# Second block's attention interleaved with its query and output projections

## The chip, the cores and the metric

One core of a Trainium2 chip runs the kernel in one launch. The metric is the device time of the whole program in microseconds (us). TensorE (PE) does the matrix products, VectorE (DVE) and ScalarE (ACT) the elementwise work, GpSimd (POOL) small set-up work, and SyncE (SP) issues the weight transfers.

## The reference, cut to what matters

The program computes two model blocks on 256 tokens of width 1024, in float32. The change lies in the second layer of the first block, a chunked band attention whose keys and values were computed from the residual stream:

```python
def chunk_band_attention(u, k_pad, v_pad, w_q, w_o, rel_bias):
    q = (u @ w_q).reshape(...)               # 16 heads of 64
    s = einsum('bqhd,bkhd->bhqk', qc, kb) * scale + bias
    p = softmax(where(valid, s, -1e30), axis=-1)
    o = einsum('bhqk,bkhd->bqhd', p, vb)
    return o.reshape(bsz, seq, B_DIM) @ w_o
# around it:
h = h + g1[:, None, :] * chunk_band_attention(...)
u = modulate(rms_norm(h, norm_ffn[layer]), sh2, sc2)
h = h + g2[:, None, :] * swiglu(u, ffn_w_in[layer], ffn_w_out[layer])
```

`g1`, `sh2`, `sc2` and `g2` come from one long row of sums, `silu(c) @ mod_w`, whose last parts are finished only just before they are used.

## The kernel before, in words

Activations are kept transposed, as 8 chunks of 128 features by 256 tokens. Every linear layer reads its weight in slots of 1 MB (1024 by 256) from a ring of six; SP issues slot n once slot n-6 is free. A slot is two pieces of 128 output features. To keep float32 accuracy a piece is split: ACT writes the high part (`hi_upto`, L739), DVE the low part as the difference (`lo_upto`, L1119), into one of four buffers; a buffer is free once the piece that held it is done on PE. A piece is then 24 matmuls on PE: for each of 8 chunks, high by high, high by low and low by high of the activations `u` (`linear`, L1750). `linear_pair` (L1763) does two pieces chunk by chunk, as `u` arrives. Two pieces share one of two PSUM banks (`lin`), which ACT or DVE drains before the next but one pair may start.

All engines run instructions in the order written; that order is set by hand. In the stretch of the change, PE does the 8 query pieces `b_q`, two row sums (L1814), then the heads, then the 8 output pieces `b_o`. DVE reads "row" slots in between (`weighted_rows`, L1180), which share the ring with the weights; the table `ROWS_AT` says behind which of the twelve slots of `kv_k`, `kv_v`, `b_q` a row slot stands.

One head is, on PE, the bias product and two score products (L2009, L2013) into bank 2 or 3; DVE takes the two maxima (L1424); ACT does the exponentials (L899); DVE takes the reciprocal and scales (L1433, L1436); PE transposes (L2024); ACT copies (L910); PE multiplies by the values (L2044, L2045) into bank 6 or 7, two heads to a chunk. `attention_pe` issues for step i: transposes of head i, scores of head i+2, values of head i-1, and what `between(i)` holds. `attention_dve` issues for step i: maxima of head i+1, scaling of head i, the drain of head i-3, `between(i)`. `attention_act`: exponentials of i, copy of i-1, drain of i-2, `between(i)`.

The eight result chunks are copied from PSUM to `qB` (ACT, L965), and once all are there, copied to the high half of `u` (ACT, L968), and subtracted for the low half (DVE, L1482). PE then starts `b_o` by `project`. At head 2 PE also turns the late row sums into columns (L1822).

Of the kernel before, what the change touches and what calls it, by code (L numbers as in the profile page):

```python
# [29 lines left out]
DC = D // P  # L30
T = 256
# [26 lines left out]
ROWS_AT = (2, 3, 4, 5, 6, 7, 8, 9)  # L58
# [123 lines left out]
def two_blocks(nc, x, c, mod_w, mod_b, norm_mix, norm_ffn, ffn_w_in, ffn_w_out, a_w_in, a_w_out, a_lb,  # L182
# [15 lines left out]
    with ExitStack() as ctx:  # L198
# [3 lines left out]
        def sem(name):  # L202
            return ctx.enter_context(nc.semaphore(name))
# [270 lines left out]
        def lo_before(k):  # L474

            return k - 12
# [30 lines left out]
        bo_hi, bo_lo = sem("bo_hi"), sem("bo_lo")  # L507
# [143 lines left out]
        def _(pool):  # L651
# [37 lines left out]
            pool.wait_ge(bo_lo, 8)  # L689
# [21 lines left out]
            pool.wait_ge(at_lo, 4)  # L711
# [17 lines left out]
        def _(act):  # L729
# [211 lines left out]
            for n, pair in enumerate(pairs("b_q")):  # L941
                result(pair)
                act.activation(qB[:, 2 * n:2 * n + 2, :], bank(pair), ACT.Copy, scale=0.125).then_inc(lin_out["act"], 1)
            drained = [0]
# [16 lines left out]
            act.wait_ge(rows_mm, 3)  # L961
            act.activation(late_rows, ps[:, 4:6, :], ACT.Copy).then_inc(rows_sb, 1)
            act.wait_ge(piece_done, LAST["b_q"] + 1)

            attention_act("B", lambda i, o: act.activation(qB[:, i // 2, :], o[:, 0:T], ACT.Copy))  # L965
            act.wait_ge(at_hi, HB // 2)
            for c_ in range(DC):
                act.activation(u[:, 0, c_, :], qB[:, c_, :], ACT.Copy).then_inc(bo_hi, 1)  # L968
# [142 lines left out]
        def _(dve):  # L1111
# [278 lines left out]
            def last_gains():  # L1390

                dve.wait_ge(gemv_col, 5)
                dve.tensor_tensor(mod[:, 80:112], ps[:, 0, 0:32], vec1[:, 80:112], ALU.add).then_inc(mod_done, 1)
# [82 lines left out]
            splits("b_q")  # L1476
            lo_upto(LAST["b_q"] + LOOKAHEAD)
            attention_dve("B", None)
            last_gains()
            for c_ in range(DC):  # L1480
                dve.wait_ge(bo_hi, c_ + 1)
                dve.tensor_tensor(u[:, 1, c_, :], qB[:, c_, :], u[:, 0, c_, :].bitcast(F32), ALU.subtract)\  # L1482
                    .then_inc(bo_lo, 1)
# [245 lines left out]
        def _(pe):  # L1729
# [267 lines left out]
            def attention_pe(kind, keys, queries, values, chunks, bias=None, between=lambda i: None):  # L1997
# [3 lines left out]
                def scores(i):  # L2001
# [3 lines left out]
                    elif i >= 2:  # L2005
                        pe.wait_ge(at_e, 2 * (a - 1))
                    o = ps[:, 2 + i % 2, :]
# [20 lines left out]
                def outputs(i):  # L2028
# [3 lines left out]
                    if k - {"B": 0, "W": 8, "X": 12}[kind] >= 2:  # L2032
                        pe.wait_ge(at_hi, k - 1)
                        if kind == "X":
                            pe.wait_ge(at_lo, lo_before(k - 1))
# [45 lines left out]
            linears(jobs["b_q"], (u_lo, 24))  # L2081
# [293 lines left out]
```

## Time and profile before

| | us |
|---|---|
| median of 3 runs | 1603.47 |
| lowest, highest | 1602.63, 1615.23 |
| the profiled execution | 1611.56 |
| its span, first to last instruction | 1609.6 |
| mean granted PE clock | 0.959 |

The profile is of one execution, which took 1611.56 us, 8.1 us more than the median. The rows from its trace give times from the start of the span. A clock of 1.00 is 2.4 GHz and 0.50 is 1.2 GHz; numbers between are means over a window that holds both.

### The profile page before, as it was taken

Reading aid. Unit: us, or ns where it says so; the run is one execution under the profiler, and the core shown is the slowest. Engines: PE = TensorE matmul, PEld = TensorE weight load, DVE = VectorE, ACT = ScalarE, POOL = GpSimd, SP = SyncE. Lnnn points to the kernel's source line nnn. Section 1 sums busy time; section 2 is a strip of 40 time slices with the busy share of each in tenths; the row PEclk is TensorE's granted clock in tenths of the full one; section 3 lists DMA queues with packets and bytes.
Section 4 is the critical chain, followed back from the end, with each engine's and each line's share of the span. In section 5 each row is a group of like instructions: output and inputs, shape, how many; then the busy total and the mean of one; then the engine's idle time right before and its main releaser. Section 6 shows DMA issues by size and latency. Waiting matters only on the chain.

```text
span 1609.6 us, 26565 instructions
## 1 busy us (share of the span) xinstructions
PE 1525.9 (95%) x11398; PEld 1250.1 (78%) x11398; DVE 712.9 (44%) x1137; ACT 566.0 (35%) x883; POOL 28.0 (2%) x47
## 2 busy tenths in 40 slices
PE   5899999899998989999999899989899999999997
PEld 3898899899998658999999778979656556556563
DVE  3657757766777425554446535644211111111110
ACT  1531244344444434544445735543111111212111
POOL 1000000000001001000000000001000000000000
PEclk8899999999989889999999879999999999999999
DMA  9668635989769403455554223716699999999992
GB/s 330 196 214 288 232 132 186 327 285 321 269 213 336 157 0 125 162 187 183 178 155 132 84 76 103 288 53 252 271 416 419 423 422 421 422 424 421 420 424 96
DMA packets 175635, 404.15 MB, mean 251 GB/s; under 512 B 5013, under 2 KB 139442, under 8 KB 163250
## 3 DMA queue, kind: packets, MB, share of 16 engines
q1 hardware_dynamic: 173504, 397.43, 66.6%
q0 software_dynamic: 1648, 5.18, 1.1%
q8 instruction: 77, 1.26, 0.3%
q10 hardware_dynamic: 386, 0.11, 0.0%
q14 instruction: 20, 0.16, 0.0%
HBM read 401.63 MB, written 1.07 MB: 250 GB/s over the span
## 4 chain that ended last, share of the span: by engine, by line
PE 87%; DVE 6%; DMA 3%; ACT 3%; issue 1%; SPq 0%; ACTq 0%; DVEq 0%
PE ps L1750 28%; PE ps L2268 14%; PE ps L2290 7%; PE ps L1981 7%; PE ps L1763 4%; PE ps L1785 4%; PE ps L2255 4%; PE ps L2300 4%; PE ps L2013 2%; PE ps L1914 2%; PE ps L1838 2%; DMA arena<-in_mod_w 2%; PE ps L1848 1%; DVE wsplit L1119 1%; PE ps L1805 1%; DMA arena<-in_b_w_q 1%
## 5 line engine op out<-in xcount | busy, mean ns | idle before, releaser
L1750 PE MATMUL ps<-u,wsplit 128*128 128x256 f32 x3912 | 485.3, 285 | 8.6 <-DVE wsplit L1119 7.1
L1750 PEld LDWEIGHTS ps<-u,wsplit 128*128 128x128 f32 x3912 | 477.0, 193 | 15.9 <-DVE wsplit L1119 8.1
L1119 DVE TENSOR_TENSOR wsplit<-arena,wsplit 128x1024 fp32r<-128x1024 f32 x258 | 312.6, 1224 | 250.4 <-ACT wsplit L739 247.4
L739 ACT ACTIVATE wsplit<-arena 128x1024 fp32r<-128x1024 f32 x258 | 270.6, 1056 | 332.2 <-PE ps L1750 161.4
L1676 DVE TENSOR_TENSOR arena<-arena,ps 128x256 f32<-128x256 f32 x32 | 13.5, 421 | 358.6 <-ACT arena L1085 358.6
L2268 PE MATMUL ps<-arena 128*64 128x256 f32 x1408 | 155.7, 379 | 0.8 <-DVE arena L1671 0.8
L2268 PEld LDWEIGHTS ps<-arena 128*64 128x64 f32 x1408 | 101.0, 137 | 60.6 <-issue 12.0
L1981 PE MATMUL ps<-hid,wsplit 128*128 128x256 f32 x1056 | 130.2, 283 | 0.3 <-DVE hid L1360 0.3
L1981 PEld LDWEIGHTS ps<-hid,wsplit 128*128 128x128 f32 x1056 | 128.2, 192 | 0.5 <-DVE hid L1360 0.5
L1091 ACT ACTIVATE arena<-ps 64x512 f32<-64x512 f32 x64 | 37.8, 591 | 154.0 <-PE ps L2290 153.2
L1763 PE MATMUL ps<-u,wsplit 128*128 128x256 f32 x528 | 73.6, 304 | 14.6 <-DVE u L1168 12.8
L1763 PEld LDWEIGHTS ps<-u,wsplit 128*128 128x128 f32 x528 | 71.3, 209 | 17.8 <-issue 17.0
L1785 PE MATMUL ps<-wsplit,u 128*128 128x256 f32 x672 | 85.0, 288 | 0.0
L1785 PEld LDWEIGHTS ps<-wsplit,u 128*128 128x128 f32 x672 | 83.0, 195 | 2.3 <-issue 2.3
L2290 PE MATMUL ps<-arena 128*64 128x512 f32 x352 | 80.4, 598 | 1.2 <-ACT arena L1088 1.2
L1085 ACT ACTIVATE arena<-ps 128x256 f32<-128x256 f32 x32 | 12.3, 383 | 174.5 <-PE ps L2268 174.5
L2268 PE MATMUL ps<-late,arena 128*64 128x256 f32 x640 | 70.8, 379 | 0.0
L2268 PEld LDWEIGHTS ps<-late,arena 128*64 128x64 f32 x640 | 45.9, 137 | 27.4 <-issue 5.7
L2255 PE MATMUL ps<-arena 128*128 128x128 f32 x512 | 63.8, 278 | 2.0 <-DVE arena L1659 2.0
L2255 PEld LDWEIGHTS ps<-arena 128*128 128x128 f32 x512 | 59.5, 192 | 7.8 <-issue 5.8
L2300 PE MATMUL ps<-arena 128*128 128x512 f32 x128 | 61.7, 605 | 1.3 <-ACT arena L1091 1.3
L2290 PEld LDWEIGHTS ps<-arena 128*64 128x64 f32 x352 | 23.3, 136 | 48.1 <-issue 45.3
(345 smaller groups left out, 1375.8 us busy)
## 6 DMA issues: line engine op xcount, KB each, us to landing
arena<-in_w SPq DMA_DIRECT2D x66, 2048.0 KB, 17.0
late<-in_w SPq DMA_DIRECT2D x30, 2048.0 KB, 17.2
arena<-in_mod_w SPq DMA_DIRECT2D x48, 1024.0 KB, 6.9
arena<-in_ffn_w_in SPq DMA_DIRECT2D x44, 1024.0 KB, 5.5
arena<-in_ffn_w_out SPq DMA_DIRECT2D x22, 1024.0 KB, 4.9
arena<-in_a_w_in SPq DMA_DIRECT2D x16, 1024.0 KB, 7.9
arena<-in_kv_mod_w SPq DMA_DIRECT2D x8, 1024.0 KB, 5.3
arena<-in_kv_w SPq DMA_DIRECT2D x8, 1024.0 KB, 7.2
```

What stands on the lines that cost most here:

```text
L739: act.activation(piece_buf(p, 0), piece_src(p), ACT.Copy).then_inc(hi_done, 1)
L1091: act.activation(y_sb[64 * k:64 * k + 64, 512 * j:512 * (j + 1)], ps[64 * j:64 * j + 64, 6, :], ACT.Copy).then_inc(m_yc, 1)
L1119: dve.tensor_tensor(piece_buf(p, 1), piece_src(p), piece_buf(p, 0).bitcast(F32), ALU.subtract).then_inc(lo_done, 1)
L1750: mm = pe.matmul(o, w_[:, k, :], u[:, x_, k, :], start=first, stop=last)
L1763: mm = pe.matmul(lin[p["out"] % 2][:, p["half"], :], piece_buf(p, lo)[:, k, :], u[:, x_, k, :], start=(at == 0 and n == 0 and p["half"] == 0),
L1785: mm = pe.matmul(lin[p["out"] % 2][:, b, :].rearrange("p (c n) -> p c n", c=2), u[:, x_, k, P * b:P * (b + 1)], wsplit[:, first_buf:first_ ...
L1838: mm = pe.matmul(o, sq[:, k, P * b:P * (b + 1)], of, start=(k == 0 and b == 0), stop=(k == DC - 1), skip_group_check=True)
L1981: mm = pe.matmul(acc[:, c_, :], piece_buf(p, lo)[:, k, P * jj:P * (jj + 1)], hid[:, fi % 2, x_, k, :], start=(i == 1 and c_ % 2 == 0 and k ...
L2255: mm = pe.matmul(ps[:, 6 + half, P * c_:P * (c_ + 1)], hn_tok[:, b, P * (4 * half + c_):P * (4 * half + c_ + 1)], sel[:, b, :], start=(b = ...
L2268: mm = pe.matmul(ps[64 * j:64 * j + 64, 0, 256 * m:256 * (m + 1)], xe[:, c_, own], w13[w_][:, m, c_, 256 * j:256 * (j + 1)], start=(c_ == ...
L2290: mm = pe.matmul(ps[64 * j:64 * j + 64, 6, :], tt[:, P * m + 64 * jk:P * m + 64 * jk + 64], w2b[w_][:, 2 * jk + m, 512 * j:512 * (j + 1)], ...
L2300: mm = pe.matmul(ps[:, 2 + 2 * b + j, :], tt[0:rows, 256 + P * b:256 + P * (b + 1)], y_sb[0:rows, 512 * j:512 * (j + 1)], start=False, sto ...
```

## The change

It has six parts.

1. `ROWS_AT` moves from slots 2 to 9 to slots 1 to 8.
2. PE does `b_q` pieces 0 and 1, the row sums, piece 2, the columns (now into the PSUM bank of `modps`), piece 3, the first two heads' scores, piece 4, and then pieces 5, 6 and 7 at steps 0, 1 and 2 of the heads. ACT drains the later query pairs inside the steps (1 and 3), and both split the weights inside them.
3. ACT writes a head pair's high part straight from PSUM to `u`, and DVE subtracts it from the same PSUM bank.
4. PE accumulates the first four `b_o` pieces by chunks: from step 5 on, each step holds the 6 matmuls of two pieces of one bank for one chunk (`out_chunk`).
5. Pieces 4 to 7 of `b_o` follow as whole pieces, with the sums of squares behind them.
6. The waits of PE and POOL on the results' semaphores are renumbered, since the heads now raise `at_lo`.

```diff
@@ -55,7 +55,7 @@
 VEC = {}
-ROWS_AT = (2, 3, 4, 5, 6, 7, 8, 9)
+ROWS_AT = (1, 2, 3, 4, 5, 6, 7, 8)
@@ -473,7 +473,7 @@
-            return k - 12
+            return k - 4
@@ -686,7 +685,7 @@
-            pool.wait_ge(bo_lo, 8)
+            pool.wait_ge(at_lo, 8)
             pool.memset(pair_ones, 0.0).then_inc(w_ms, 1)
@@ -708,7 +707,7 @@
-            pool.wait_ge(at_lo, 4)
+            pool.wait_ge(at_lo, 12)
             pool.memset(turned, 0.0).then_inc(m_const, 1)
@@ -938,9 +937,30 @@
             operand_hi("mix1", lambda c_: mod[:, 64 + c_:65 + c_], LAST["kv_v"])
-            for n, pair in enumerate(pairs("b_q")):
+            def queries(pair):
+                n = pairs("b_q").index(pair)
                 result(pair)
                 act.activation(qB[:, 2 * n:2 * n + 2, :], bank(pair), ACT.Copy, scale=0.125).then_inc(lin_out["act"], 1)
+            queries(pairs("b_q")[0])
+            act.wait_ge(rows_mm, 3)
+            act.activation(late_rows, ps[:, 4:6, :], ACT.Copy).then_inc(rows_sb, 1)
+            queries(pairs("b_q")[1])
+            def amid_b(i):
+                if i == 0:
+                    hi_upto(jobs["b_q"][7]["w"])
+                elif i in (1, 3):
+                    queries(pairs("b_q")[(i + 3) // 2])
+                elif i == 4:
+                    hi_upto(jobs["b_o"][3]["w"])
+            def out_hi(i, o):
+                if i == 1:
+                    act.wait_ge(piece_done, LAST["b_q"] + 1)
+                return act.activation(u[:, 0, i // 2, :], o[:, 0:T], ACT.Copy)
             drained = [0]
@@ -958,14 +978,7 @@
-            act.wait_ge(rows_mm, 3)
-            act.activation(late_rows, ps[:, 4:6, :], ACT.Copy).then_inc(rows_sb, 1)
-            act.wait_ge(piece_done, LAST["b_q"] + 1)
-            attention_act("B", lambda i, o: act.activation(qB[:, i // 2, :], o[:, 0:T], ACT.Copy))
-            act.wait_ge(at_hi, HB // 2)
-            for c_ in range(DC):
-                act.activation(u[:, 0, c_, :], qB[:, c_, :], ACT.Copy).then_inc(bo_hi, 1)
+            attention_act("B", out_hi, amid_b)
             hi_upto(jobs["b_o"][0]["w"] + LOOKAHEAD)
@@ -1390,7 +1403,7 @@
                 dve.wait_ge(gemv_col, 5)
-                dve.tensor_tensor(mod[:, 80:112], ps[:, 0, 0:32], vec1[:, 80:112], ALU.add).then_inc(mod_done, 1)
+                dve.tensor_tensor(mod[:, 80:112], modps[:, 80:112], vec1[:, 80:112], ALU.add).then_inc(mod_done, 1)
                 dve.wait_ge(mod_done, 11)
@@ -1473,14 +1486,20 @@
                 dve.tensor_copy(memT[:, 4 * b:4 * b + 4, :], acc[:, 4 * b:4 * b + 4, :]).then_inc(x_tc, 1)
-            splits("b_q")
-            lo_upto(LAST["b_q"] + LOOKAHEAD)
-            attention_dve("B", None)
+            lo_upto(jobs["b_q"][1]["w"])
+            weighted_rows(jobs["rows_kv"][-1])
+            lo_upto(jobs["b_q"][6]["w"])
             last_gains()
-            for c_ in range(DC):
-                dve.wait_ge(bo_hi, c_ + 1)
-                dve.tensor_tensor(u[:, 1, c_, :], qB[:, c_, :], u[:, 0, c_, :].bitcast(F32), ALU.subtract)\
-                    .then_inc(bo_lo, 1)
+            def amid_b(i):
+                if i == 0:
+                    lo_upto(jobs["b_q"][7]["w"])
+                elif 2 <= i < 5:
+                    lo_upto(jobs["b_o"][i - 1]["w"])
+            attention_dve("B", lambda i, o: dve.tensor_tensor(
+                u[:, 1, i // 2, :], o[:, 0:T], u[:, 0, i // 2, :].bitcast(F32), ALU.subtract), amid_b)
@@ -1994,7 +2013,8 @@
             ffn_pe(0, "ffn0")
-            def attention_pe(kind, keys, queries, values, chunks, bias=None, between=lambda i: None):
+            def attention_pe(kind, keys, queries, values, chunks, bias=None, between=lambda i: None,
+                             arriving=lambda i: None):
@@ -2004,6 +2024,7 @@
                         pe.wait_ge(at_e, 2 * (a - 1))
+                    arriving(i)
                     o = ps[:, 2 + i % 2, :]
@@ -2031,8 +2052,8 @@
                         pe.wait_ge(at_hi, k - 1)
-                        if kind == "X":
-                            pe.wait_ge(at_lo, lo_before(k - 1))
+                        if kind != "W":
+                            pe.wait_ge(at_lo, k - 1 if kind == "B" else lo_before(k - 1))
                     pt = pt_sb[:, i % 2, :]
@@ -2078,10 +2099,14 @@
                     mm.then_inc(x_tp, 1)
-            linears(jobs["b_q"], (u_lo, 24))
+            linear_pair(jobs["b_q"][0:2], (u_lo, 24))
             pe.wait_ge(x_tc, 2)
...
             row_sums(3, ps[:, 5, :]).then_inc(rows_mm, 1)
+            linear(jobs["b_q"][2])
+            columns(late_rows[:, 0, :], 3, modps[:, 80:96])
+            columns(late_rows[:, 1, :], 3, modps[:, 96:112]).then_inc(gemv_col, 1)
+            linear(jobs["b_q"][3])
@@ -2093,21 +2118,48 @@
-            wait_out(pe, jobs["b_q"][-1])
+            def out_chunk(c_, n):
+                pair = pairs("b_o")[n]
+                if c_ == 0:
+                    pe.wait_ge(lo_done, pair[1]["w"] + 1)
+                    pe.wait_ge(lin_out[pair[0]["engine_before"]], pair[0]["turn_before"])
+                pe.wait_ge(at_lo, c_ + 1)
+                for p in pair:
+                    for m, (lo, x_) in enumerate(((0, 0), (0, 1), (1, 0))):
+                        mm = pe.matmul(lin[p["out"] % 2][:, p["half"], :], piece_buf(p, lo)[:, c_, :], u[:, x_, c_, :],
+                                       start=(c_ == 0 and m == 0 and p["half"] == 0),
+                                       stop=(c_ == DC - 1 and m == 2), skip_group_check=True)
+                    if c_ == DC - 1:
+                        mm.then_inc(piece_done, 1)
+            def amid_b(i):
+                if i < 3:
+                    linear(jobs["b_q"][5 + i])
+                elif i >= 5:
+                    out_chunk((i - 5) // 2, (i - 5) % 2)
+            def queries_there(i):
+                if i % 4 == 0:
+                    wait_out(pe, jobs["b_q"][i // 2])
             pe.wait_ge(b_rel, 96)
...
             half = lambda t_, i: t_[64 * (i % 2):64 * (i % 2) + 64, i // 2, :]
-            def late_columns(i):
-                if i == 2:
-                    columns(late_rows[:, 0, :], 3, ps[:, 0, 0:16])
-                    columns(late_rows[:, 1, :], 3, ps[:, 0, 16:32]).then_inc(gemv_col, 1)
             attention_pe("B", lambda i, k: half(kB, i), lambda i, k: half(qB, i),
-                         lambda i, b, m: vB[:, b, 64 * i:64 * i + 64], 1, lambda i: biasB[:, i, :], late_columns)
-            pe.wait_ge(mod_done, 12)
-            project("b_o", "ffn1", (bo_lo, 0), follows=jobs["gate1_0"])
+                         lambda i, b, m: vB[:, b, 64 * i:64 * i + 64], 1, lambda i: biasB[:, i, :], amid_b,
+                         queries_there)
+            for c_ in (6, 7):
+                for n in range(2):
+                    out_chunk(c_, n)
+            for n in (2, 3):
+                for p in pairs("b_o")[n]:
+                    linear(p)
+                sums("ffn1", [0, 1] if n == 2 else [2])
+            warm(jobs["gate1_0"], 3)
+            sums("ffn1", [3])
+            warm(jobs["gate1_0"], 1)
             ffn_pe(1, "ffn1")
@@ -2212,7 +2264,7 @@
                          lambda i, b, m: vX[:, b, T * i + P * m:T * i + P * (m + 1)], 2)
-            pe.wait_ge(at_lo, 4)
+            pe.wait_ge(at_lo, 12)
             project("co", "moe", None, follows=jobs["co"][4:])
```

PE's order from the query projection to step 0, before (L1763 and L1750 are `b_q`, L1814 row sums, L2009 and L2013 scores, L2024 transposes):

```order
L1763 MATMUL ps<-u,wsplit 128x256 x48
L1750 MATMUL ps<-u,wsplit 128x256 x144
L1814 MATMUL ps<-arena,ones 32x512 x4
L1814 MATMUL ps<-late,ones 32x512 x4
L2009 MATMUL ps<-arena 128x384
L2013 MATMUL ps<-arena 128x128
L2013 MATMUL ps<-arena 128x256
L2009 MATMUL ps<-arena 128x384
L2013 MATMUL ps<-arena 128x128
L2013 MATMUL ps<-arena 128x256
L2024 MATMUL ps<-ident,arena 128x128 x3
```
and with the change (L1782 and L1769 are `b_q`, L1833 row sums, L1841 columns, L2030 and L2034 scores, L2045 transposes):

```order
L1782 MATMUL ps<-u,wsplit 128x256 x48
L1833 MATMUL ps<-arena,ones 32x512 x4
L1833 MATMUL ps<-late,ones 32x512 x4
L1769 MATMUL ps<-u,wsplit 128x256 x24
L1841 MATMUL ps<-ident,sq 128x4 x8
L1769 MATMUL ps<-u,wsplit 128x256 x24
L2030 MATMUL ps<-arena 128x384
L2034 MATMUL ps<-arena 128x128
L2034 MATMUL ps<-arena 128x256
L2030 MATMUL ps<-arena 128x384
L2034 MATMUL ps<-arena 128x128
L2034 MATMUL ps<-arena 128x256
```
The pieces that stood together are now apart, with row sums, columns and scores between them. PE's order from step 4 to step 6 with the change (L2065 and L2066 are the values, L2130 the output chunks):

```order
L2045 MATMUL ps<-ident,arena 128x128 x3
L2030 MATMUL ps<-arena 128x384
L2034 MATMUL ps<-arena 128x128
L2034 MATMUL ps<-arena 128x256
L2065 MATMUL ps<-arena 64x256
L2066 MATMUL ps<-arena 64x128
L2045 MATMUL ps<-ident,arena 128x128 x3
L2030 MATMUL ps<-arena 128x384
L2034 MATMUL ps<-arena 128x128
L2034 MATMUL ps<-arena 128x256
L2065 MATMUL ps<-arena 64x256
L2066 MATMUL ps<-arena 64x128
```
Step 4 has no filling; from step 5 on six matmuls of the output projection stand behind the values. ACT's order in steps 3 and 4 with the change (L898 exponentials, L909 copies, L962 the drain into `u`, L738 splits, L943 the drain of a query pair):

```order
L898 ACTIVATE arena,small<-ps,small 128x128
L898 ACTIVATE arena,small<-ps,small 128x256
L909 ACTIVATE arena<-ps 128x384
L962 ACTIVATE u<-ps 128x256
L738 ACTIVATE wsplit<-arena 128x1024 x2
L943 ACTIVATE arena<-ps 128x512
L898 ACTIVATE arena,small<-ps,small 128x128
L898 ACTIVATE arena,small<-ps,small 128x256
L909 ACTIVATE arena<-ps 128x384
L738 ACTIVATE wsplit<-arena 128x1024
```
ACT drains heads 0 and 1 into `u` before it splits the output pieces. SP's order of transfers, before and with the change (`in_mod_w` are the row slots; it begins with the last slots of `kv_v`):

```order
L608 DMA arena<-in_kv_w 128x8x256
L608 DMA arena<-in_mod_w 128x2048
L608 DMA arena<-in_kv_w 128x8x256
L608 DMA arena<-in_mod_w 128x2048
L608 DMA arena<-in_b_w_q 128x8x256
L608 DMA arena<-in_mod_w 128x2048
L608 DMA arena<-in_b_w_q 128x8x256
L608 DMA arena<-in_mod_w 128x2048
L608 DMA arena<-in_b_w_q 128x8x256 x2
```
```order
L607 DMA arena<-in_kv_w 128x8x256
L607 DMA arena<-in_mod_w 128x2048
L607 DMA arena<-in_kv_w 128x8x256
L607 DMA arena<-in_mod_w 128x2048
L607 DMA arena<-in_kv_w 128x8x256
L607 DMA arena<-in_mod_w 128x2048
L607 DMA arena<-in_b_w_q 128x8x256
L607 DMA arena<-in_mod_w 128x2048
L607 DMA arena<-in_b_w_q 128x8x256 x3
```
One row slot more now stands ahead of each of the first two `b_q` slots; the third follows the second at once.

## Rows read from the trace of the kernel before

**Rows 1.** Windows: length; busy PE, PEld, DVE, ACT, POOL; PE clock; DMA share; GB/s.
```profile
547.84:576.87 29.03, 26.94 (x77) 15.90 (x78) 6.22 (x25) 7.22 (x27) 0.00 (x0) 0.53 0.00 1
576.87:608.22 31.35, 25.55 (x117) 14.07 (x117) 11.18 (x45) 14.06 (x52) 0.00 (x0) 1.00 0.00 1
```

**Rows 2.** Waits of PE from 543 to 613: total us, times, longest.
```profile
PE ps L2024 <- DVE arena L1436: 9.3, 12, 1.4
PE ps L1763 <- DVE u L1482: 1.5, 1, 1.5
```

**Rows 3.** Chain of waits, a late head: start, us, engine, tile, line.
```profile
576.87 0.55 PE ps L2024 x3
577.42 0.65 PE ps L2009 x2
578.06 0.86 PE ps L2013 x4
...
579.02 0.62 DVE small L1424 x2
579.64 0.08 DVE small L1433
...
579.75 0.56 DVE arena L1436 x2
...
608.77 0.57 PE ps L2044 x2
609.35 0.22 PE ps L2045 x2
```

**Rows 4.** Chain of waits: transposes of two early heads, and the late columns.
```profile
553.04 0.90 PE ps L2024 x3
...
558.27 0.87 PE ps L2024 x3
...
563.47 3.51 PE ps L1822 x16
```

**Rows 5.** Chain of waits: first query pair, row sums, output pairs, sums of squares.
```profile
515.75 8.00 PE ps L1763 x48
...
541.23 1.85 PE ps L1814 x16
...
612.96 5.99 PE ps L1763 x48
...
631.35 0.79 PE ps L1838 x8
632.14 5.86 PE ps L1750 x48
```

**Rows 6.** The page, costliest groups: the weight splits on DVE and ACT.
```profile
L1119 DVE TENSOR_TENSOR wsplit<-arena,wsplit 128x1024 fp32r<-128x1024 f32 x258 | 312.6, 1224 | 250.4 <-ACT wsplit L739 247.4
L739 ACT ACTIVATE wsplit<-arena 128x1024 fp32r<-128x1024 f32 x258 | 270.6, 1056 | 332.2 <-PE ps L1750 161.4
```

**Rows 7.** Lines by form, 577 to 608: the drain of two heads on ACT.
```profile
L965 ACT ACTIVATE arena<-ps 128x256 f32<-128x256 f32 x4 | 1.5, 383 | 7.2 <-PE ps L2045 7.2
```

**Rows 8.** Timeline after output pieces 0 and 1: start, us, instruction.
```profile
620.92 0.87 DVE L1189 SCALAR_TENSOR_TENSOR h<-ps,mod,h 128x256 f32<-128x256 f32 x2
621.83 0.63 ACT L768 ACTIVATE sq<-h 128x512 f32<-128x512 f32 x1 [2.08 <-DVE h L1189]
622.48 1.28 ACT L779 ACT_TABLE_LOAD   x1
```

**Rows 9.** Windows of the weight transfers, columns as in group 1.
```profile
467.00:472.00 5.00, 5.00 (x44) 5.00 (x43) 2.98 (x4) 3.13 (x4) 0.00 (x0) 1.00 0.63 210
480.00:506.00 26.00, 26.00 (x219) 26.00 (x218) 18.30 (x12) 9.07 (x11) 3.49 (x4) 1.00 1.04 348
```

**Rows 10.** Chain of waits ahead of the query projection.
```profile
495.30 16.40 DMA arena<-in_b_w_q
```

**Rows 11.** A window of PE alone: length, busy, clock, DMA share, GB/s.
```profile
546.00:548.00 2.00, 0.63 (x4) 0.91 0.00 0
```

More of the change, by code:

```diff
@@ L506, in two_blocks @@
         x_n = sem("x_n")
-        bo_hi, bo_lo = sem("bo_hi"), sem("bo_lo")
         flip = part(12288, P)
```

## The prediction

> **What bounds the kernel now.** I read the page first: its busy times name PE as the engine that works nearly throughout, so time is won only where PE waits or runs slowly. Then the windows by stage [rows 1], for the clock, and the chain of waits, for what PE does. The stretch of the change begins with the query projection at 515.75 and ends with the last output piece at 632.14 + 5.86 = 638.00 [rows 5]: 122.25 us. In its middle the reader should see two kinds of heads. From 547.84 to 576.87 the clock is 0.53, so PE is at 1.2 GHz nearly throughout; from 576.87 to 608.22, nine heads in 31.35 us (3.48 each), it is at 2.4 GHz [rows 1].
>
> The chain of waits shows what a late head is made of [rows 3]: transposes 0.55, scores 0.65 + 0.86, then DVE 0.62 + 0.08 + 0.56 with some 0.16 of handing over, during which PE has only the values, 0.57 + 0.22. PE works 2.85 of 3.48 us and waits 0.65. The waits of PE say the same: 9.3 us in 12 waits for the scaled probabilities, 1.5 us for the last chunk [rows 2].
>
> Bookkeeping at full clock: query pieces 541.23 - 515.75 = 25.5 (left as measured), row sums 1.85 [rows 5], columns 3.51 / 2 = 1.76, measured at half clock [rows 4], 16 heads of 2.85 = 45.6, four output pairs of 5.86 = 23.4, two sums of squares of 0.79 = 1.6 [rows 5]. That is 99.7. With the waits of 10.8 it is 110.5; the other 11.8 of the 122.25 are the low clock.
>
> **The change, part by part.** No matmul goes or comes; the 99.7 stays. Counting what PE waits for then:
>
> *Steps 0 to 2.* A query piece of 5.86 / 2 = 2.93 [rows 5] stands behind each head, more than the 0.65 that PE waited: these waits go. The second query pair needs its drain before head 4's scores; its last piece is done before the heads, so it costs nothing.
>
> *The end of step 2: a new wait.* ACT's drain of heads 0 and 1 writes `u`, so it waits for the last query piece, which PE does at the end of step 2. The split of output piece 1 stands behind that drain on ACT, and DVE's step 2 ends with the low part of that piece, ahead of the maxima of head 4 and the scaling of head 3. PE's next instruction is the transposes of head 3. After the last query piece it therefore waits for the drain 0.38 [rows 7], the splits 1.06 and 1.22 [rows 6], and DVE's 0.62 + 0.08 + 0.56 [rows 3]: 3.92, with four handings-over 4.1 us. Behind it on ACT are also the exponentials of head 4 and query pair 3, needed only by head 12. If ACT had the split done earlier, 1.3 would be left; if clock or queues add, 5.
>
> *Steps 3 and 4.* Nothing fills them: 2 x 0.65 = 1.3.
>
> *Steps 5 on.* Six matmuls of an output chunk, 6 x 0.122 = 0.73, replace the wait: 2.85 + 0.73 = 3.58 a step against 3.48, and PE never waits. DVE was busy 11.18 and ACT 14.06 of 31.35 us there [rows 1], so a drain of 0.4 on each every second step stays beside PE; that DVE now reads the result from PSUM changes little, since it adds from PSUM at 0.87 / 2 too [rows 8]. The eight copies by way of `qB` go, all off PE but the last. The end wait of 1.5 also goes: the last chunk's drain of 0.4 + 0.4 is hidden by the two chunks of number 6.
>
> *After the last chunk.* Output piece 4 needs the buffer of piece 0, which ends nine matmuls (1.1) before the chunks do. Split 1.06 + 1.22, then DVE adds the first pair, 0.87 [rows 8], which frees the bank: 3.15 - 1.1 = 2.1 of wait. Piece 5 comes worse: ACT first takes the squares (0.63) and a table load (1.28, with its 0.2 activation) before its split [rows 8]. Counted from the last chunk that is 2.1 + 2.1 + 1.06 + 1.22 = 6.5, while piece 4 ended at 5.0: 1.5 more. Before, pieces 2 and 3 covered both; their cover is what accumulating by chunks uses up. Zero is the low end of this pair of waits, 5 the high one.
>
> *One row slot earlier.* It puts one more 1 MB transfer ahead of the first two query slots, and PE waits for the second one [rows 10]. From 480 to 506 the DMA engines are full, at 348 GB/s, so a slot takes 3.0 us; but from 467 to 472 their share was 0.63, which leaves 1.85 for it [rows 9]. I take 3.0 - 1.85 = 1.2, bounds 0 and 3.0. The row tile's DVE work moves to where DVE was free, and the late row sums come about when PE asks for them: 0, at most 1. The Trainium skill, page "DMA: Bandwidth & Descriptors", section "Issuing engines are not separate DMA queues", says that transfers issued by different engines run on the same 16 DMA engines and interleave. The full share above, while POOL's bias tables move beside SP's slots, agrees. By that rule alone nothing of the added slot would be absorbed, and the term would be 3.0, the sum 1.8 us later.
>
> Of the feed-forward part behind, nothing moves: its first slots are issued as early as before, and POOL's constants wait for the last result as before. 0.
>
> Idle then is 4.1 + 1.3 + 2.1 + 1.5 = 9.0 against 10.8. With the 1.2: 99.7 + 9.0 + 1.2 = 109.9, so 12.4 less than 122.25 if the clock never falls, nearly all of it the clock's.
>
> *The clock.* Before, it fell about when PE had waited 1.4 us: the window 546 to 548 has PE busy 0.63 us and a clock of 0.91 [rows 11]. The wait of 4.1 is three times as long, so I expect a fall there. At 1.2 GHz a head takes 5.2 us (553.04 to 558.27 [rows 4]), 1.7 more than 3.5, and a step with a chunk 5.2 + 1.46 = 6.7, 3.1 more than 3.58. Before, heads alone stayed low for some 27 us (29.03 at 0.53, [rows 1]); so steps 3 and 4 cost 3.4. Then come dense matmuls in each step, and I guess that one such step, 3.1, is enough: 6 in round numbers, between 0 and the whole rest (rival C). After the last chunk the waits of 2.1 and 1.5 may bring another fall: one dense pair costs 8.00 - 5.99 = 2.0 more when it begins low, by the first query pair against the first output pair [rows 5]; I take 1.5.
>
> Sum: -12.4 + 6 + 1.5 = -4.9. Against the profiled execution of 1611.56 that gives 1606.7. That execution lies 8.1 above the median of the runs. If what made it slow lies elsewhere the changed kernel can be 8.1 faster too; I give this, and that it falls on the median, a fifth, and predict **1605**, 0.1% over the median.
>
> **The rivals.**
> - A, *the clock does not matter after all*: either it rises at once in step 3, or the two waits are shorter because the chunks' bank and buffers come free earlier. 1611.6 - 12.4 = 1599; with the 8.1 elsewhere, 1591. For it: nine heads in a row with waits of 0.65 never let the clock fall. Against: one wait of 1.4 did. The faster end needs both the clock and the 8.1, and another 4 us of waits gone: 1587 or less.
> - B, *a low stretch as long as the old one*, 11.8 for the 6: 1612 to 1613. It would mean that chunks do as little for the clock as heads.
> - C, *the low clock through all remaining heads*. Its place is step 3, its price 3.4 + 9 x 3.1 = 31 and some 5 for the last steps and chunks: 1599 + 36 + 1.5 = 1637, 2% slower. It decides from about five steps beyond the fourth. For it: PE was busy 26.94 of the 29.03 us in which the clock stayed low [rows 1], so a busy PE is not enough. Against: that stretch ended by itself, and the new steps hold dense pieces. [...]
> - D, *the interleaving does not hide what it should*: ACT's drain of query pair 2 stands ahead of the exponentials of head 2 and waits for the piece of step 0. If each of the steps 0 to 2 lost 2 us to such order, 1611. It stands beside 2.93 us of PE's own work per step, so I hold it unlikely.
>
> **Numbers.** Forecast 0.50 (1598 to 1612), A 0.20, B 0.13, C 0.10, D 0.07. What this kernel can tell from no change is about 1%, 16 us: faster is below 1587.4, slower above 1619.5. Faster 0.14: half of A, where all three come together, and 0.04 of the forecast, should its waits be absent as well as its clock loss. Slower 0.12: C, and 0.02 for B and D together going further. Same 0.74. The range leaves out C and A's lowest half, 0.2 in all: 1588 to 1615.
>
> **What would show it.** In the profile after: a wait of PE of about 4 us for DVE's scaling behind the last query piece, with the clock at 0.5 after it; waits of 0.65 in two steps only; steps of 3.6 us with chunks and no idle; two waits of 2.1 and 1.5 for splits behind the last chunk; the first query matmul about 1.2 later against the end of the value pieces. It is wrong if ACT splits output piece 1 before the last query piece ends, if the clock stays at 1.00 through a wait of 4 us, or if it does not return once chunks run.

## The result

| | before | after |
|---|---|---|
| median, 20 runs each on the same chip, us | 1609.51 | 1601.47 |
| lowest, highest | 1601.48, 1619.02 | 1598.6, 1608.56 |
| the profiled execution, span | 1611.56, 1609.6 | 1605.1, 1603.2 |
| mean granted clock of it | 0.959 | 0.962 |

The ratio after to before is 0.9949, with a 95% interval of [0.9934, 0.9965]: half a per cent faster, a small gain, but one that 20 runs each settle. The forecast was as good as no change (0.1% over) against 1603.47, the median of three runs. That number was not typical. The kernel before ran 79 more times beside the experiments below, with a median of 1610.98; so the profiled execution of 1611.56 was an ordinary one, and two of the three runs were of the quicker group (below). The profiled execution of after, 1605.1, is the third slowest of its 20.

**The heads.** The waits of PE between 513 and 640 in the profile after (total us, times, longest), to be held against [rows 2]:

```profile
PE ps L1782 <- DVE u L1181: 4.8, 1, 4.8
PE ps L2045 <- DVE arena L1449: 3.9, 1, 3.9
PE ps L1769 <- DVE h L1202: 2.3, 1, 2.3
PE ps L1769 <- DVE wsplit L1132: 1.2, 1, 1.2
```

The twelve waits for the scaled probabilities have become one of 3.9, and the 1.5 ahead of the output pieces is gone. The other two, 2.3 and 1.2, are new and stand behind the last chunk. (The first, 4.8, lies ahead of the query pieces.) What makes the 3.9 is in the chain of waits:

```profile
552.47 3.08 PE ps L1769 x24
555.92 1.06 ACT wsplit L738
557.03 1.11 issue
558.14 0.61 DVE small L1437 x2
558.86 0.56 DVE arena L1449 x2
559.47 0.90 PE ps L2045 x3
560.37 1.28 PE ps L2030 x2
561.65 1.58 PE ps L2034 x4
...
570.77 0.95 PE ps L2030 x2
571.72 0.85 PE ps L2034 x4
...
573.36 0.90 PE ps L2130 x6
574.26 0.33 PE ps L2045 x3
```

The last query piece ends at 555.55 (552.47 + 3.08). ACT drains the heads' results and splits output piece 1 (to 556.98). The 1.11 called issue is DVE's split of the low part, 1.22 from 557.00 in the timeline; only then come maxima and scaling, and PE turns at 559.47. The transposes then take 0.90 for three, where a turn at full clock takes 0.55 [rows 3]: the clock has fallen. It is back within step 5: the scores there begin slow (0.95 for two where half clock takes 1.28) and end at 0.85 for four. From step 6 on a step is 574.26 to 577.80, 3.54, without idle.

Windows (columns as in [rows 1], whose two rows they answer; the last answers to [rows 11]):

```profile
556.00:560.00 4.00, 0.54 (x3) 0.54 (x4) 2.97 (x7) 3.31 (x8) 0.00 (x0) 0.70 0.08 23
560.00:568.00 8.00, 8.00 (x21) 4.13 (x19) 3.25 (x8) 2.84 (x7) 0.00 (x0) 0.50 0.45 138
568.00:572.00 4.00, 4.00 (x13) 2.13 (x13) 1.25 (x5) 1.57 (x6) 0.00 (x0) 0.59 0.65 226
572.00:600.00 28.00, 28.00 (x153) 18.35 (x152) 11.28 (x44) 12.32 (x44) 0.00 (x0) 1.00 0.00 1
...
546.00:548.00 2.00, 2.00 (x14) 1.67 (x15) 1.87 (x6) 0.92 (x4) 0.00 (x0) 1.00 0.00 0
```

The reader is to see a low stretch of some 12 us (560 to about 571.5, and the idle just before) where before has one of 27, and PE busy 28.00 of 28 with the chunks.

**Around them.** Ends of the stretch, in the chain, to be held against [rows 5]:

```profile
515.05 8.19 PE ps L1782 x48
...
607.35 2.72 PE ps L2130 x21
610.15 1.07 ACT wsplit L738
611.32 1.23 DVE wsplit L1132
612.54 0.80 DVE h L1202 x2
613.48 0.54 issue
614.01 1.28 ACT L778
615.51 0.96 ACT wsplit L738
616.49 1.23 DVE wsplit L1132
617.77 3.14 PE ps L1769 x24
620.91 1.68 PE ps L1857 x16
622.59 5.86 PE ps L1769 x48
```

Behind the last chunk stand the split 1.07 + 1.23 and the add 0.80, then the table load of 1.28 and the next split. The last output pair ends at 628.45, before at 638.00. From the first query matmul to there it is 113.4 us against 122.25: 8.85 less. The whole span is only 6.4 shorter: the query projection began 0.7 earlier, and the part behind the last output pair took 3.15 longer, with code that the change leaves alone. That execution lost 2.4 us more clock outside this stretch than before's did (table of executions below). The weight transfers, against [rows 9] and [rows 10]:

```profile
467.00:472.00 5.00, 5.00 (x44) 5.00 (x44) 4.24 (x5) 3.35 (x4) 0.00 (x0) 1.00 0.73 226
480.00:506.00 26.00, 26.00 (x219) 26.00 (x218) 18.09 (x12) 9.36 (x12) 4.09 (x5) 1.00 1.05 362
...
495.09 15.91 DMA arena<-in_b_w_q
```

These rows don't tell whether the added slot is absorbed. The share from 467 to 472 differs between executions with the same order of slots (0.65 in e2 and 0.15 in e8, 0.30 to 0.98 in those with the new order), and the 348 GB/s were low for the old order (359 in e2, 355 in e8, against 358 to 362 with the new). What PE waited ahead of the query pieces is nearer to the point: 5.3, 4.4 and 4.3 us in the three profiled executions with the old order, 4.8 to 6.7 in the nine with the new (mean 5.4), so about 0.8 more, with overlap. The splits are as in [rows 6]: 1222 ns on DVE, 1056 on ACT.

### The profile page after: what moved, and what is told of

It is laid out like the page before. It is cut to its first block, busy times and chain, and to the rows that moved or that the text cites. A ratio compares the mean times of both kernels' runs of the same rounds, so it can differ in the third digit from the quotient of the medians.

```text
span 1603.2 us, 26560 instructions
## 1 busy us (share of the span) xinstructions
PE 1523.4 (95%) x11398; PEld 1249.0 (78%) x11398; DVE 712.9 (44%) x1137; ACT 562.7 (35%) x875; POOL 28.4 (2%) x47
## 3 DMA queue, kind: packets, MB, share of 16 engines
HBM read 401.63 MB, written 1.07 MB: 251 GB/s over the span
## 4 chain that ended last, share of the span: by engine, by line
PE 88%; DVE 5%; DMA 3%; ACT 2%; issue 1%; SPq 0%; ACTq 0%; DVEq 0%
PE ps L1769 27%; PE ps L2320 14%; PE ps L2342 7%; PE ps L2000 7%; PE ps L1804 4%; PE ps L2307 4%; PE ps L2352 4%; PE ps L1782 4%; PE ps L1857 2%; PE ps L1933 2%; PE ps L2034 2%; DMA arena<-in_mod_w 2%; PE ps L1867 2%; DVE wsplit L1132 1%; PE ps L1824 1%
## 5 line engine op out<-in xcount | busy, mean ns | idle before, releaser
L1769 PE MATMUL ps<-u,wsplit 128*128 128x256 f32 x3864 | 479.0, 285 | 13.2 <-DVE wsplit L1132 9.4
L1769 PEld LDWEIGHTS ps<-u,wsplit 128*128 128x128 f32 x3864 | 469.6, 193 | 22.7 <-DVE wsplit L1132 13.1
L1132 DVE TENSOR_TENSOR wsplit<-arena,wsplit 128x1024 fp32r<-128x1024 f32 x258 | 312.2, 1222 | 250.9 <-ACT wsplit L738 247.3
L738 ACT ACTIVATE wsplit<-arena 128x1024 fp32r<-128x1024 f32 x258 | 270.3, 1056 | 325.7 <-PE ps L1769 157.0
L1782 PE MATMUL ps<-u,wsplit 128*128 128x256 f32 x480 | 66.7, 304 | 11.8 <-DVE u L1181 11.5
L1782 PEld LDWEIGHTS ps<-u,wsplit 128*128 128x128 f32 x480 | 64.8, 209 | 14.2 <-issue 13.9
```

The source lines that it names most:

```text
L738: act.activation(piece_buf(p, 0), piece_src(p), ACT.Copy).then_inc(hi_done, 1)
L1132: dve.tensor_tensor(piece_buf(p, 1), piece_src(p), piece_buf(p, 0).bitcast(F32), ALU.subtract).then_inc(lo_done, 1)
L1769: mm = pe.matmul(o, w_[:, k, :], u[:, x_, k, :], start=first, stop=last)
L1782: mm = pe.matmul(lin[p["out"] % 2][:, p["half"], :], piece_buf(p, lo)[:, k, :], u[:, x_, k, :], start=(at == 0 and n == 0 and p["half"] == 0),
```

## The experiments

Two readings had to be told apart. **The clock**: what before loses is mostly one long low stretch in most of its executions, and the change makes it short. **The waits**: the gain is the removed idle time itself, or one of the change's other parts (results split from PSUM, the earlier row slot). All ran beside the kernel before; ratios are to it, n is the number of runs. The experiments ran in three groups, each on a chip of its own (e1 to e4, e5 to e8, e9 and e10), and a ratio is to before's runs of its group. The ratios are not quotients of the medians: before's runs fall in two groups, its median sits in the slower one, and by medians e2 would be 0.995 and e3 0.990.

| kernel | median us (n) | ratio, 95% interval | median clock of its runs |
|---|---|---|---|
| before, in all experiments | 1610.98 (79) | | 0.959 |
| after | 1601.47 (20) | 0.9949 [0.9934, 0.9965] | 0.965 |
| e1 row slots alone | 1611.0 (12) | 1.0024 [0.9999, 1.005] | 0.9585 |
| e8 split from PSUM alone | 1610.94 (12) | 1.0006 [0.9981, 1.0031] | 0.959 |
| e2 before, idle matmuls | 1603.21 (12) | 0.9971 [0.9947, 0.9996] | 0.968 |
| e4 after, idle matmuls | 1599.89 (12) | 0.9938 [0.9914, 0.9962] | 0.967 |
| e3 after, early split | 1595.12 (12) | 0.9925 [0.9897, 0.9953] | 0.967 |
| e5 chunks behind the heads | 1610.31 (12) | 0.9995 [0.9974, 1.0016] | 0.9635 |
| e6 queries ahead of the heads | 1604.08 (12) | 0.996 [0.9939, 0.9981] | 0.9635 |
| e7 both early splits | 1595.05 (6) | 0.9913 [0.9884, 0.9943] | 0.967 |
| e10 the same once more | 1595.07 (8) | 0.9909 [0.9876, 0.9942] | 0.968 |
| e9 e7 and idle matmuls | 1594.22 (8) | 0.9902 [0.9866, 0.9939] | 0.968 |

One execution of each kernel was profiled, and its trace separates this stretch from the rest of the program. "Stretch" is the time from the first query matmul to the end of the last output pair. "Clock lost" is the sum of length times (1 - clock) over windows of 20 us, inside 500 to 660 and outside; 3.4 of it, about the start of the query projection, is in every execution.

| profiled execution | stretch, us | clock lost, 500 to 660 | elsewhere |
|---|---|---|---|
| before | 122.3 | 17.0 | 48 |
| e1 (heads as before) | 111.2 | 3.4 | 50 |
| e8 (heads as before, but for the drains) | 115.2 | 8.6 | 50 |
| e2 | 112.1 | 3.4 | 48 |
| after | 113.4 | 10.2 | 51 |
| e4 | 109.3 | 3.4 | 51 |
| e3 | 105.8 | 3.4 | 55 |
| e5 | 119.1 | 11.8 | 45 |
| e6 | 112.8 | 8.6 | 50 |
| e7 | 105.7 | 5.2 | 49 |
| e10 (the same kernel) | 104.4 | 3.4 | 53 |
| e9 | 106.9 | 5.2 | 46 |

So the 8.9 us between before and after in this stretch can be split: before's low stretch cost 11.1 (122.3 against e1's 111.2), after's cost 4.1 (113.4 against e4's 109.3), and with no low clock the two differ by 1.9. Each of these is one execution. What is lost elsewhere goes from 45 to 55 with no order by kernel. A run's mean clock alone therefore doesn't say whether this stretch was low in it.

**e1, the row slots alone.**

```diff
-ROWS_AT = (2, 3, 4, 5, 6, 7, 8, 9)
+ROWS_AT = (1, 2, 3, 4, 5, 6, 7, 8)
```

> The kernel before with the row slots one earlier and nothing else. Theory 1 (the gain is the low clock's shorter stretch and the waits between heads; the row slots give nothing): 0 to 1 us against before, first query matmul within 1 us of 515.75. Rival (the row slots are part of the gain, since the first query matmul of the changed kernel came 0.7 us earlier and not 1.2 later): 1 to 3 us faster. My prediction's own term: 1.2 us slower.

1.0024: nothing, or up to half a per cent of loss. So the gain is not from here. Its profiled execution showed something else. Here the heads' code is that of before, word for word, and these are its windows:

```profile
548.00:576.00 28.00, 23.03 (x114) 13.55 (x115) 9.04 (x37) 11.71 (x42) 0.00 (x0) 1.00 0.00 1
576.00:608.00 32.00, 26.01 (x143) 16.82 (x142) 13.59 (x49) 15.44 (x50) 2.75 (x7) 1.00 0.02 3
```

Against [rows 1]: clock 1.00 in the first window, where it was 0.53, with the same wait of 1.4 ahead of it. This execution took 1604.9, the fastest of the twelve. So the low stretch of before comes in some executions and not in others. Its first query matmul came at 516.74, within the 1 us that was expected, but on the late side, after a wait of 6.7.

**e8, the results' split straight from PSUM alone.**

```diff
-            attention_act("B", lambda i, o: act.activation(qB[:, i // 2, :], o[:, 0:T], ACT.Copy))
-            act.wait_ge(at_hi, HB // 2)
-            for c_ in range(DC):
-                act.activation(u[:, 0, c_, :], qB[:, c_, :], ACT.Copy).then_inc(bo_hi, 1)
+            attention_act("B", lambda i, o: act.activation(u[:, 0, i // 2, :], o[:, 0:T], ACT.Copy))
...
-            attention_dve("B", None)
+            attention_dve("B", lambda i, o: dve.tensor_tensor(
+                u[:, 1, i // 2, :], o[:, 0:T], u[:, 0, i // 2, :].bitcast(F32), ALU.subtract))
```

> The kernel before with part 3 of the change alone: the heads' results are split straight from PSUM, the output projection still follows the heads. Theory 1 (this part gives only what little the last chunk's copies were): the wait of 1.5 us before the output projection becomes 0.9 to 1.0, so 0 to 1 us faster than before, and the low clock as in before. Rival (its drains on DVE delay the scaling and lower the clock further): 1 to 4 us slower.

1.0006: nothing. Its waits show why the 1.5 of [rows 2] did not simply go:

```profile
PE ps L2018 <- DVE arena L1433: 9.9, 13, 1.4
PE ps L1757 <- DVE gain L1392: 1.2, 1, 1.2
```

PE waits there for the late gains as well, which DVE does behind the last drain; the copies' wait had hidden most of that one. The low clock was expected "as in before"; it came, behind a wait of 1.4 as there, but lasted ten us and not 27:

```profile
552.00:562.00 10.00, 8.56 (x24) 4.72 (x23) 2.48 (x10) 2.81 (x10) 0.00 (x0) 0.53 0.01 2
```

**e2, before with idle matmuls.** Four matmuls (eight rows of 0.24 us) whose result nobody reads, ahead of PE's first wait in the heads.

```diff
+                if i == -1:
+                    warm(jobs["b_o"][0:2], 4)
```

> The kernel before with four idle-value matmuls (some 1.8 us) between the scores of the first two heads and the transposes of the first, where PE waited 1.4 us and the clock fell. Theory 1 (most of the difference is the clock that this wait loses): no low stretch from 547 on, the heads take 3.48 each from the first, and the time falls by 8 to 11 us, as much as or more than the whole change gives. Rival (the clock falls whatever fills that wait, or the low stretch is not there in most executions): within 2 us of before, and the low stretch still begins within the first heads.

In the chain, and the windows to be held against [rows 1]:

```profile
543.52 1.92 PE ps L1848 x8
545.44 0.33 PE ps L2024 x3
```
```profile
548.00:576.00 28.00, 23.42 (x116) 13.82 (x116) 9.32 (x38) 12.07 (x43) 0.00 (x0) 1.00 0.00 1
576.00:608.00 32.00, 26.66 (x156) 18.53 (x156) 13.82 (x46) 15.09 (x46) 4.13 (x11) 1.00 0.12 33
```

The first of two waits of 1.4 is filled and the second remains (9.2 us in 13; e1, with both, has 10.6 in 14). The low stretch is gone from this execution, and 0.29% [0.04, 0.53] of the time from the runs: 1.9 us of useless work bought 4.7. By the ratio that is less than the 8 to 11 forecast and more than the rival's 2, with an interval that reaches both; by the medians it is 7.9. Eight of its twelve runs had a clock of 0.965 or more, against 19 of the 79 of before; the other four lie at 0.960 to 0.962, so it does not help in every execution. That is the clock's part, made by hand without any other part of the change.

**e4, after with idle matmuls behind the last query piece.**

```diff
                     linear(jobs["b_q"][5 + i])
+                    if i == 2:
+                        warm(jobs["b_o"][0:2], 8)
```

> The changed kernel with eight idle-value matmuls (some 3.7 us) behind the last query piece, in the wait of 3.9 us. The wait itself stays. Theory 1 (the wait is what lowers the clock): steps 3 to 5 at 2.4 GHz, 4.2 - 1.3 = about 3 us less than the changed kernel. Rival (steps 3 and 4 lower the clock by themselves): no difference, 0 to 1 us more.

```profile
556.00:562.00 6.00, 5.53 (x33) 4.73 (x32) 3.05 (x7) 3.70 (x9) 0.00 (x0) 1.00 0.12 20
562.00:572.00 10.00, 8.71 (x43) 4.99 (x42) 5.88 (x19) 5.33 (x17) 0.00 (x0) 1.00 0.59 198
```

The turn of PE comes as late as before (3.9 after the piece's end), but at full clock, and the waits of some 0.6 that half clock had covered are there again (1.8 in 3). From PE's turn to the start of step 6 it is 10.7 us (561.39 to 572.10) where after took 14.8 (559.47 to 574.26): 4.1 less, those waits included. The runs show less, 0.1% under after and within the intervals. Perhaps many of after's executions lose less clock than the profiled one; that isn't shown.

**e3, the split of output piece 1 earlier on ACT**, so that it doesn't stand behind the drain that waits.

```diff
+                elif i == 2:
+                    hi_upto(jobs["b_o"][1]["w"])
```

> The changed kernel with ACT's split of output piece 1 in step 2 of the heads, ahead of the drain of heads 0 and 1 that waits for the last query piece. Theory 1: the wait of 3.9 us behind the last query piece goes, the clock stays at 2.4 GHz through steps 3 to 5, which then take 3.5 each: 3.9 + 4.2 - 1.3 = about 7 us less than the changed kernel, some 15 less than before. Rival (the clock falls in steps 3 and 4 anyway, since they have nothing between the heads): only the wait goes, about 4 us less than the changed kernel.

```profile
PE ps L1771 <- DVE h L1204: 2.3, 1, 2.3
PE ps L2047 <- DVE arena L1451: 2.0, 2, 1.3
PE ps L1771 <- DVE wsplit L1134: 1.2, 1, 1.2
```

The 3.9 has become 2.0 in two waits, the clock stays at 1.00 through them, and of the single additions to the changed kernel it gives most: 0.9925. So the wait at the end of step 2 was the order on ACT, as the prediction had it (it put what would be left at 1.3; it is 2.0). By medians it is 6.4 us under after, near the 7 expected, by the ratios 0.24%, 3.9 us.

**e5, all chunks behind the heads.**

```diff
-                elif i >= 5:
-                    out_chunk((i - 5) // 2, (i - 5) % 2)
...
-            for c_ in (6, 7):
+            for c_ in range(DC):
```

> The changed kernel with all 16 output chunks behind the heads, none between them. Theory 1 (chunks fill the waits of 0.65 and bring the clock back): steps 5 to 13 take 3.48 each, 12 chunks of 0.73 to 0.91 move onto the path, some 8 us; and the low clock that begins in the wait behind the last query piece lasts as long as in the kernel before, some 27 us and not 12, which costs 4 to 7 more: 12 to 15 us slower than the changed kernel. Rival (the clock comes back by itself after about 12 us): 8 us slower, the low stretch 12 us long.

```profile
556.00:571.00 15.00, 12.98 (x35) 6.97 (x35) 7.00 (x19) 6.27 (x19) 0.00 (x0) 0.54 0.44 140
571.00:600.00 29.00, 23.60 (x109) 12.97 (x108) 12.16 (x48) 12.61 (x46) 0.00 (x0) 1.00 0.00 1
```

The chunks inside the steps are worth 8.8 us of median (1610.31 less 1601.47), 7.4 by the ratios and 5.7 by the two profiled stretches: without them PE waits 9.7 us in ten waits instead of 3.9 in one. But the clock came back without them, as long after PE's turn (some 12 us in both). My guess that dense chunks bring it back is not borne out: they are not needed for it. e8 above and e6 below show the same, with low stretches of ten us that ended where no chunk had run.

**e6, all query pieces ahead of the heads.**

```diff
+            for p in jobs["b_q"][4:]:
+                linear(p)
...
-                if i < 3:
-                    linear(jobs["b_q"][5 + i])
-                elif i >= 5:
+                if i >= 5:
```

ACT and DVE have the splits and drains of these pieces ahead of the heads too.

> The changed kernel with all eight query pieces ahead of the heads; chunks from step 5 on as they are. The wait of 3.9 us goes with the interleaving, but waits of 1.4 before head 0 and 0.65 at steps 0 to 4 come back: about 4.7 for 3.9, so 1 us slower if the clock does the same. Theory 1 (in most executions the clock falls at the first head's wait, and chunks bring it back only from step 5 on): a low stretch of some 24 us from the first head in most executions, 10 for 4.2: 5 to 7 us slower than the changed kernel. Rival (clock losses are alike): 0 to 2 slower.

0.996, 2.6 us over after (0.1% by the ratios, within the intervals), where theory 1 had 5 to 7 and the rival 0 to 2. Its heads begin as those of before: a wait, and a low stretch, of ten us and not the 24 of theory 1:

```profile
548.00:558.00 10.00, 8.56 (x25) 4.59 (x25) 3.06 (x11) 2.89 (x11) 0.00 (x0) 0.54 0.01 2
```

It ended some 12 us ahead of the first chunk, which ran at 571.47. So the four query pieces amid the heads are worth little as they stand (they trade waits of 4.8 us for the one of 3.9), the output chunks more.

**e7, e10 and e9, the best.** e7 adds to e3 the splits of output pieces 5 and 6 ahead of the squares and the table load on ACT (the expectation of e9 calls them the next matrix's third and fourth piece; they belong to `b_o`); e10 is e7 again; e9 adds four idle matmuls behind the last query piece.

```diff
-                        hi_upto(jobs[job][2 * n + 1]["w"] + LOOKAHEAD)
+                        hi_upto(jobs[job][max(2 * n + 1, 3 if name == "ffn1" else 0)]["w"] + LOOKAHEAD)
```

> The changed kernel with output piece 1 split in step 2, as in the third experiment, and with the splits of output pieces 5 and 6 ahead of the squares and the table load. The last chunk's second wait of 1.2 us goes: 1.2 less than the third experiment, some 8 less than the changed kernel. Rival (ACT then delays the squares, and the sums of squares wait in its place): same as the third experiment.

> The kernel with both early splits once more, unchanged, since only six runs of it were timed: its 0.9913 [0.9884, 0.9943] should be repeated, 0.990 to 0.993. If the six runs were lucky ones, it comes to 0.9925, what the first of the two early splits gives alone, and the second split is worth nothing.

> The kernel after with both early splits (of the second output piece, and of the next matrix's third and fourth piece) and four idle matmuls of 128x128x256 behind the last query piece. Theory (what a wait costs is mostly the clock it loses, and only what is left of the wait beyond the idle matmuls): the early splits leave waits of 1.3 and 0.7 us there, too short to lose the clock in most executions; four matmuls of 0.12 each fill 0.5 of them. So within 0.1% of the kernel with both early splits alone: ratio 0.991 to 0.992, clock the same. Rival (the clock still falls in many executions of the kernel with both early splits): then these matmuls bring 0.2 to 0.3% more, ratio 0.988 to 0.9895, and the mean clock of the runs is 0.002 higher.

The chain of e7 behind the last chunk, against that of after above, and then the same output pair in e10, the same kernel:

```profile
604.80 0.80 DVE h L1204 x2
605.60 0.14 issue
605.73 7.29 PE ps L1771 x48
613.02 1.68 PE ps L1859 x16
```
```profile
608.74 5.98 PE ps L1771 x48
```

The second wait (1.2) is gone. The pair takes 7.29 in e7 and 5.98 in e10, since the clock fell behind the wait of 2.3 in the one and not in the other. 0.9913 was repeated as 0.9909, beside 0.9902 with the idle matmuls, a difference of 0.1% within the intervals: little low clock was left there to win. (Those four matmuls took 1.73 us in e9's trace, and not the 0.5 of the expectation; PE's waits went from 2.0 to 1.3.) These beat both kernels, by 0.9% and 0.4%; how much of it is the second split can't be told (0.9925 lies within the intervals).

## Why the prediction was wrong

**Its working, against the profile after.**

| step | predicted | measured |
|---|---|---|
| wait behind the last query piece | 4.1 | 3.93 |
| steps 3 and 4, waits of 0.65 and low clock together | 5.2 each | 5.22, 5.20, no wait |
| clock: steps 3, 4 and one more | 3.4 + 3.1, called 6 | 5.22 + 5.20 + 4.37 - 3 x 3.53 = 4.2 |
| a step with a chunk | 3.58, no idle | 3.53, no idle (chunk 0.91 for 0.73, transposes 0.33 for 0.55) |
| waits behind the last chunk | 2.1, 1.5 | 2.34, 1.19 |
| clock behind them | 1.5 | 0 here; 1.4 in e7 |
| the stretch, all terms but the row slot | 99.7 + 9.0 + 7.5 = 116.2 | 113.4 |
| row slot earlier | +1.2 | first query matmul 0.7 earlier here; e1 +0.2% [0, +0.5%]; wait ahead of it 0.8 more on average |
| the rest of the program | 0 | 3.15 longer |

The places, their order and the lengths of the waits came out. Against the profiled execution the sum gave 1606.7, and the profiled execution of after took 1605.1. That this is so close is luck: the stretch came 2.8 us shorter than the sum, the query projection began 0.7 earlier instead of 1.2 later, and the rest of the program, put at 0, took 3.15 longer. The length of a step with a chunk is luck too: two wrong parts cancel.

**The step that failed** is the last: "That execution lies 8.1 above the median of the runs", of which I gave a fifth away and forecast 0.1% over the median of 1603.47. The 8.1 were not this execution's bad luck; over 99 runs the median is near 1610 to 1611. The same sum against it is 1606, 0.3% faster: the right direction, though still short of the interval, 0.35 to 0.66% faster. From a median of three whose lowest and highest are 12.6 apart I should have taken the profiled execution, on which the sum was built, as the level.

**The size that failed** is the clock. I priced the change's clock loss at 7.5; it was 4.2. Steps 3 and 4 came out as forecast: their waits of 0.65 don't show while half clock makes PE the bound, but the price per step, 1.7 over 3.5, had them in it. What came less is the step after them, 0.8 and not the 3.1 of a whole step, since the clock came back within it and not because of its dense piece (e5), and the pair behind the last chunk, 0 and not 1.5. On the other side the prediction took before's low stretch as given, 11.8 in every execution; e1 shows an execution without it, and its stretch is 11.1 shorter.

**Where the gain is.** Before's runs gather in two groups by clock: 38 of 79 at 0.957 to 0.959 and 17 at 0.965 to 0.967. The 24 at 0.963 or more have a median of 1602.9, the 55 below it 1611.6. The 13.6 us of clock that before's low stretch lost (17.0 less 3.4) are 0.008 of the span, the distance between the groups; that it is this stretch that parts them is an estimate from one trace, since the rest of the program spreads by nearly as much (45 to 55). After's 20 runs lie from 0.960 to 0.967. At the same clock the two kernels are close: at 0.965 before took 1602 to 1605 us (8 runs) and after 1599.0 to 1601.8 (3); at 0.967 before 1599 to 1604 (8) and after 1598.6 to 1599.9 (3). A straight line through before's 79 runs falls by 1.24 us for each 0.001 of clock, and after's runs lie on average 2.4 us under it. So, as an estimate, some 2.4 us are the shorter waits (10.8 to 7.4, less what the row slot may cost), and the other 5.2 of the 7.6 between the means go with the clock. The traces split it alike: 1.9 us of waits, and 11.1 less 4.1 of clock in the pair that was profiled. e2 shows it by intervention: idle matmuls against the low stretch, and nothing else, give 0.29 of the 0.51%, with wide intervals; e4, after without its own, is 3.3 us under e2.

**The rivals.** A (the clock doesn't matter) came nearest to the number, not to the mechanism: it fell behind the wait of 4 us, as forecast. B and C didn't happen, D neither: steps 0 to 2 show no wait.

**Open.** Why a wait of 1.4 loses the clock in one execution (before, e6, e8) and not in another (e1), and why the low stretch lasts 27 us in before and ten in e8 and e6; no difference was found that explains it. How often before's stretch is low can't be counted, since only three executions with its heads were profiled, two of them low. Whether the row slot costs anything: e1's interval goes from 0 to 8 us.

## What to carry over

When a kernel's runs spread, list each with its mean clock before trusting a median of three: two groups can mean a stretch whose clock is lost in some executions only, and then what a change wins depends on how often that happens and not on one profile. Look for the one long wait ahead of a low stretch and ask what stands ahead of it in the same queue; moving one split (e3) gave more than moving four query pieces amid the heads (e6). Filling a wait with useless matmuls wins the clock back (e4), but taking the wait away wins more (e3, 4.8 us of median under e4 in the same group of runs).

## What the runs showed of the hardware

- The time of an execution follows its mean granted clock: over 79 runs of before the correlation is -0.97, with 1620 us at 0.953 and 1600 at 0.968.
- The same code with the same wait of 1.4 us ran on at 1.00 (e1) or fell to 0.50 for 27 us [rows 1]; behind the same wait e6 and e8 were low for ten us. The waits of 3.9 us in after and in e5 were each followed by a low stretch of some 12 us. A wait of 2.3 us behind the last chunk lowered the clock in e5, e7 and e9 and not in after, e3, e4, e6 and e10.
- In before, e5, e6 and e8 the clock came back while PE ran heads and no chunk, as the scores' durations in the chain show (e5: 0.94 us for two of them at 569.32 where half clock takes 1.28).
- At half clock the heads' waits nearly vanish: PE busy 26.94 of 29.03 there [rows 1], 23.03 of 28 for the same code at full clock (e1).
